# Last value tile in two halves, modulation chunk rows and flips one tile sooner in branch units, modulation straight from the centred tile

## What is computed

```
for l in range(DEPTH):                                    # DEPTH = 2
    sh1, sc1, g1, sh2, sc2, g2 = split(silu(c) @ w_mod[l] + b_mod[l], 6)      # and the same of c_ctx
    a = x * (1 + sc1) + sh1
    f, nq, nk, nv, cq, ckv, kr, g = split(a @ w_in[l])
    ys = [fourier_mix(f), neighbourhood_attention(nq, nk, nv), mla(cq, ckv, kr)]
    m = sum_i(sigmoid(g_i) * (ys_i @ w_branch[l, i])) @ w_out[l]
    x = layer_norm(ALPHA * x + (1 + g1) * m, ln1_g[l], ln1_b[l])
    f = swiglu(x * (1 + sc2) + sh2)
    x = layer_norm(ALPHA * x + (1 + g2) * f, ln2_g[l], ln2_b[l])
```

## Time and profile before

| | |
|---|---|
| median of the 3 runs shown | 2131.55 us (2127.8, 2150.82, 2131.55) |
| profiled execution, its own time | 2127.88 us |
| its span, granted clock (mean) | 2126.1 us, 0.97 |
| PE busy | 1969.0 us (93%), 12468 matmuls |
| PEld (weight loads) | 1626.4 us (76%) |
| VectorE busy | 1281.8 us (60%), 2174 instructions |
| ScalarE busy | 848.6 us (40%), 1366 instructions |
| GpSimd busy | 129.0 us (6%) |
| DMA | 332.07 MB, mean 156 GB/s |

### The profile page before, as it was taken

How to read it: one execution, slowest core, us unless ns; L and a number is a source line. 1 busy time by engine, 2 the same in 40 slices (tenths; PEclk the granted TensorE clock), 3 DMA queues, 4 the chain that set the end, 5 groups by cost and what they waited for, 6 DMA issues and landing times.

```text
span 2126.1 us, 32028 instructions
## 1 busy us (share of the span) xinstructions
PE 1969.0 (93%) x12468; PEld 1626.4 (76%) x12468; DVE 1281.8 (60%) x2174; ACT 848.6 (40%) x1366; POOL 129.0 (6%) x110
## 2 busy tenths in 40 slices
PE   5999989998999999999898988989997899988998
PEld 3776657546768788887687664879997889987998
DVE  6512454564447567677634566666667777666775
ACT  4422353253234122222433445354445754444444
POOL 0000000000030001204000000020111100000000
PEclk9999999999999999999999999999997999998999
DMA  9642513105553556546465140856662446652664
GB/s 328 188 139 82 175 40 94 50 1 181 176 184 123 203 183 200 196 158 218 129 216 167 62 134 2 283 194 196 199 196 90 150 146 193 189 167 81 205 193 137
DMA packets 280758, 332.07 MB, mean 156 GB/s; under 512 B 13190, under 2 KB 229692, under 8 KB 280508
## 3 DMA queue, kind: packets, MB, share of 16 engines
q1 hardware_dynamic: 268608, 323.05, 46.6%
q10 hardware_dynamic: 12028, 7.32, 1.3%
HBM read 329.31 MB, written 1.05 MB: 155 GB/s over the span
## 4 chain that ended last, share of the span: by engine, by line
PE 75%; DVE 8%; issue 6%; DMA 5%; ACT 4%; POOL 1%; SPq 1%; DVEq 0%; ACTq 0%; POOLq 0%
PE ps L550 20%; PE ps L551 19%; PE ps L552 19%; PE ps L1341 3%; DVE SL L509 2%; PE ps L1367 2%; PE ps L368 2%; DMA RAW<-in_w_in 2%; PE ps L1351 2%; ACT SH L503 1%; DMA RAW<-in_w_out 1%; PE ps L947 1%; PE ps L1576 1%; DMA EARLY<-in_w_mod 1%; DMA RAW<-in_w_branch 1%
## 5 line engine op out<-in xcount | busy, mean ns | idle before, releaser
L509 DVE TENSOR_TENSOR SL<-RAW,SH 128x1024 fp32r<-128x1024 f32 (+2 forms) x448 | 524.5, 1174 | 431.1 <-ACT SH L503 426.4
L550 PE MATMUL ps<-AB,SH 128*128 128x256 f32 (+1 forms) x1984 | 644.6, 325 | 40.2 <-DVE AB L1077 22.6
L551 PE MATMUL ps<-AB,SH 128*128 128x256 f32 (+1 forms) x1984 | 637.2, 321 | 0.0
L552 PE MATMUL ps<-AB,SL 128*128 128x256 f32 (+1 forms) x1984 | 636.7, 321 | 0.0
L503 ACT ACTIVATE SH<-RAW 128x1024 fp32r<-128x1024 f32 (+2 forms) x448 | 443.6, 997 | 423.4 <-PE ps L552 269.0
L550 PEld LDWEIGHTS ps<-AB,SH 128*128 128x128 f32 x1984 | 378.2, 191 | 94.4 <-issue 34.5
L552 PEld LDWEIGHTS ps<-AB,SL 128*128 128x128 f32 x1984 | 378.9, 191 | 29.2
L551 PEld LDWEIGHTS ps<-AB,SH 128*128 128x128 f32 x1984 | 378.1, 191 | 27.5
L550 PE MATMUL ps<-HH,SH 128*128 128x256 f32 (+1 forms) x992 | 304.5, 307 | 3.5 <-DVE HL L779 1.6
L551 PE MATMUL ps<-HL,SH 128*128 128x256 f32 (+1 forms) x992 | 302.4, 305 | 0.0
L552 PE MATMUL ps<-HH,SL 128*128 128x256 f32 (+1 forms) x992 | 302.4, 305 | 0.0
(11 more groups left out here) (286 smaller groups left out, 2176.8 us busy)
## 6 DMA issues: line engine op xcount, KB each, us to landing
SIDE<-in_w_mod SPq DMA_DIRECT2D x45, 2048.0 KB, 8.0
RAW<-in_ffn_w SPq DMA_DIRECT2D x64, 1024.0 KB, 5.4
RAW<-in_w_in SPq DMA_DIRECT2D x44, 1024.0 KB, 6.1
RAW<-in_w_ffn_gate SPq DMA_DIRECT2D x22, 1024.0 KB, 9.0
RAW<-in_w_ffn_up SPq DMA_DIRECT2D x22, 1024.0 KB, 5.4
RAW<-in_w_ffn_down SPq DMA_DIRECT2D x16, 1024.0 KB, 5.8
RAW<-in_w_branch SPq DMA_DIRECT2D x24, 512.0 KB, 3.5
RAW<-in_w_out SPq DMA_DIRECT2D x8, 1024.0 KB, 6.7
```

The costliest lines, as they stand in the source:

```text
L509: e.tensor_tensor(SL[:, m, 0:kt, :], RAW[p][:, 0:kt, o:o + P], SH[:, m, 0:kt, :].bitcast(F32), ALU.subtract).then_inc(K.up("weight_low"), 1)
L550: e.matmul(ps, SH[:, m, k, :], xh, start=k == 0, stop=False)
L551: e.matmul(ps, SH[:, m, k, :], xl, start=False, stop=False)
L552: ins = e.matmul(ps, SL[:, m, k, :], xh, start=False, stop=k == self.kt - 1)
```

## The change

Five edits in three groups.

- `Values`: token tile 3 is made in two halves of 256 columns, as tile 0 is. A new semaphore, `values_half`, is signalled after the first half, and ScalarE then splits the next unit's weight tiles 0 and 1 before it copies tile 3 of the values; tiles 2 and 3 follow it.
- Branch units: rows stand before tile 2 (`rows_tile = 2`), and VectorE's flip before it waits for tile 2's products. In the opening, the turn of chunk 2 and the rows of chunk 3 move from before (0, 1) to before (2, 0), and the turn of chunk 3 from before (2, 1) to before (0, 1).
- Norms that write both: A is computed from the centred tile NT, not from X, and ScalarE does so before it writes X. For that the preparation folds gain and bias in: scale = gain x scale', shift = bias x scale' + shift', in DER rows 2, 3 and 8, 9: instead of one VectorE instruction per stream, four. The buffer of NT is still given back after X is written.

```diff
@@ class Unit
+        rows_tile = 3
@@ def pe(self, e, K):
-                if self.side and (m, k) == (3, 0) and not self.by_k:
+                if self.side and (m, k) == (self.rows_tile, 0) and not self.by_k:
                     self.side.pe_rows(e, K, 0)
@@ def dve(self, e, K):
-                if self.side and m == self.side.flip_at and not (self.by_k or self.hold):
+                if self.side and m == (self.rows_tile if self.rows_tile < 3 else self.side.flip_at) and not (self.by_k or self.hold):
                     self.side.flip(e, K, 0)
@@ class Values
-                halves = [(0, 2), (2, 4)] if t == 0 else [(0, 4)]
+                halves = [(0, 2), (2, 4)] if t in (0, 3) else [(0, 4)]
...
+                    if (t, m0) == (3, 0):
+                        ins.then_inc(K.up("values_half"), 1)
                 ins.then_inc(K.up("products"), 1)
...
         def act(self, e, K):
-            for m in range(4):
+            for m in range(3):
                 e.wait_ge(sem["products"], K.at("products", m + 1))
                 self.read_act(e, K, m)
-            for m in range(4):
+            e.wait_ge(sem["values_half"], K.at("values_half", 1))
+            for m in (0, 1):
+                self.nxt.split_act(e, K, m, 2)
+            e.wait_ge(sem["products"], K.at("products", 4))
+            self.read_act(e, K, 3)
+            for m in (2, 3):
                 self.nxt.split_act(e, K, m, 2)
@@ class Branch
+        rows_tile = 2
@@ class Norm, def act
                 t = NT[:, k % 2, c0:c1]
+                if self.to == "a":
+                    if k >= 2:
+                        e.wait_ge(sem["input_low"], K.at("input_low", k - 1))
+                    if self.split and k == 0:
+                        e.wait_ge(sem["dve_done"], K.at("dve_done"))
+                    for s, c in enumerate(range(c0, c1, SEQ)):
+                        last = c + SEQ == c1
+                        at = c - c0
+                        e.activation(A32[:, k % 2, c:c + SEQ], t[:, at:at + SEQ], ACT.Identity,
+                                     bias=self.sh(s, k), scale=self.sc(s, k)) \
+                            .then_inc(K.up("modulated" if last else "act_done"), 1)
                 if self.write_x:
                     e.activation(X[:, k, c0:c1], t, ACT.Identity, bias=self.b(k), scale=self.g(k)) \
                         .then_inc(K.up("x_normed"), 1)
...
-                if self.to == "a":
...
-                    if self.write_x:
-                        e.wait_ge(sem["x_normed"], K.own("x_normed"))
-                        src = X[:, k, c0:c1]
...
+            if self.write_x:
+                e.wait_ge(sem["x_normed"], K.own("x_normed"))
@@ class Opening, def pe_between
-            if (m, k) == (0, 1):
+            if (m, k) == (2, 0):
                 self.turn(e, K, 2)
                 self.rows_of(e, K, 3)
-            if (m, k) == (2, 1):
+            if (m, k) == (0, 1):
                 self.turn(e, K, 3)
@@ 
-    def prep_scales(alpha, mat, chunk_sc, streams):
+    def prep_scales(alpha, mat, chunk, streams, t=slice(0, 8)):
         def f(e, K):
             e.wait_ge(sem["side_added"], K.own("side_added"))
             for s in range(streams):
-                e.tensor_scalar(DER[:, 2 + s, :], mod(mat, chunk_sc, s), 1.0, 1.0 / alpha, ALU.add, ALU.mult) \
+                e.tensor_scalar(DER[:, 2 + s, t], mod(mat, chunk + 1, s)[:, t], 1.0, 1.0 / alpha, ALU.add, ALU.mult) \
                     .then_inc(K.up("dve_done"), 1)
+            e.wait_ge(sem["dve_done"], K.own("dve_done"))
+            for s in range(streams):
+                e.tensor_tensor(DER[:, 8 + s, t], DER[:, 2 + s, t], DER[:, 1, t], ALU.mult).then_inc(K.up("dve_done"), 1)
+            e.wait_ge(sem["dve_done"], K.own("dve_done"))
+            for s in range(streams):
+                e.tensor_tensor(DER[:, 8 + s, t], DER[:, 8 + s, t], mod(mat, chunk, s)[:, t], ALU.add) \
+                    .then_inc(K.up("dve_done"), 1)
+                e.tensor_tensor(DER[:, 2 + s, t], DER[:, 2 + s, t], DER[:, 0, t], ALU.mult).then_inc(K.up("dve_done"), 1)
```

34 lines of the change are left out of this document (9 added, 25 removed).

## The result

The changed kernel takes 2124.69 us in the median of 16 runs (2110.93 to 2134.12). The kernel before, beside it on the same chips, takes 2141.62 us (16 runs, 2127.8 to 2150.95). The ratio is 0.9919, 95% interval 0.9897 to 0.994: 17 us faster. That is 0.8%, less than the 1% from which the prediction would have called it faster. The forecast said 19.1 us, 0.9%. The difference came as forecast, but the time did not: 2124.7 us lies above the range, 2103 to 2120, because the kernel before is slower than the 2128 to 2132 us from which I subtracted.

A forecast was written before the change was run, and what follows sets the result against it. TensorE was taken to bound the kernel (three quarters of the last-ending chain). +0.4 - 2 x 2.5 - 2 x 1.7 - 5.7 - 3.7 - 1.7 = -19.1 us; forecast 2110 (-0.9%), range 2103 to 2120.

The forecast's parts named there:

- Values, -8.4: Tile 3 in halves ends a 2.78 us wait before the gate, costs 0.30; with low clock, 4.2 per layer, 8.4 both.
- echo: Low clock on PE behind a wait, as at 149 to 153 behind Values (0.58), counted at 1.7 us each.
- Branch turns, -5.7: Two branch-unit turns, at 529.38 and 570.46, lose their waits of 2.43 and 3.31 us for the flip: 5.7 us gained.
- Norms, -3.7 and -1.7: A ahead of X gains 0.84, 1.7 and 1.2 us in three norms, together 3.7; clock behind tail waits 1.7 more.
- The half of the echoes that I counted there: Low clock behind two norm-tail waits, 1.7 us each; waits shorten but stay, so 1.7 of 3.4 was counted.
- Opening, +0.4: Six more small VectorE operations make the opening 0.70 us later; one removed wait comes back, leaving a cost of 0.4.
- The 0.27 us that I took back: Opening: one wait of 0.27 us at 52.55 that the earlier turn and rows of chunk 3 would let VectorE remove.
- the NT ring: Rival: norms' centring buffer freed too late, a tile takes 3.3 instead of 2.39 us; +3, 2131; chance 0.04.
- blocked halves: Rival: splits at Values' halves blocked by a bank or RAW, losing 0.6 instead of gaining 8.4; -10, 2118; chance 0.03.
- the second Values' gain given back in layer 1: Rival: layer 1's gate and branch units wait for weights, swallowing 4.2 us; -15, 2114; chance 0.23 with the low-clock rival.
- the low clock moves instead of leaving: Rival: low clock at Values and norm tails only moves, so 3.4 + 1.7 drop out; -14, 2115; 0.23 with the give-back.
- the base: Time the gain was subtracted from: the profiled 2127.88, giving 2108.8; the shown median, 3.7 higher, would give 2112.4.

The follow-up runs named there:

- e5: The kernel before with only the branch units' edit (rows before tile 2, flip before tile 2's products): 2123.11 us, ratio to before 0.9947.
- e6: The changed kernel with the branch units' flip back behind tile 2's products on VectorE, rows still before tile 2: 2119.91 us, ratio to before 0.9915.
- e4: The kernel before with only the norms' part and the opening's moved turns and rows: 2136.06 us, ratio to before 0.9967.
- e8: The changed kernel with the opening's VectorE split of the third weight tile moved behind the first cast: 2120.33 us, ratio to before 0.9916.
- e2: The changed kernel run once more with no edit: 2126.16 us, ratio to before 0.9892.
- e7: The changed kernel with ScalarE writing X ahead of A in each norm tile, A still computed from NT: 2125.04 us, ratio to before 0.9942.
- e3: The kernel before with only Values' token tile 3 in halves and the early splits: 2124.0 us, ratio to before 0.9908.

## Why the prediction was right in the difference and wrong in the time

*Values, -8.4.* Right: 95.8 - 87.4 (8.1 if e5, with its one echo missing, is averaged in). The halves cost 0.31 us in layer 0 and 0.16 in layer 1 (the stretch that ends at the turn went from 24.60 to 24.91 and from 24.60 to 24.76), where I put 0.30 for each. Two waits of 2.78 and two clock echoes are gone.

*Branch turns, -5.7.* Right, 5.9 or 5.3 by the reference, and by the mechanism named (e6). I had too little here: in three of the six profiles that still have these waits, the low clock follows them and costs 1.4 to 4.3 us more ("behind": 50.0, 52.7 and 52.9 in place of 48.6). My remark that these waits have no low stretch behind them was true of one execution. It isn't true of the kernel.

*Norms, -3.7 and -1.7.* Right in the sum: 367.8 to 362.5 is 5.3 us, echoes included, against 5.4. It is spread otherwise than I had it (1.1, 1.6 and 2.5 us in the three), and the tail of layer 0's second norm keeps its echo. In after the clock is low for longer there than the 4 us of the earlier trace rows, and PE still stops for VectorE:

```profile
1030.49 0.38 PE L551 MATMUL ps<-AB,SH 128*128 128x256 f32 x1 [1.76 <-DVE AB L1086]
...
1030.50:1038.00 7.50, 6.99 (x33) 6.67 (x33) 4.19 (x5) 4.69 (x8) 0.00 (x0) 0.54 0.80 167
```

The half of the echoes that I counted there was a guess, and it shows in no row.

*Opening, +0.4.* The chain of small operations was 0.68, forecast 0.70, and it reached PE: from the start of VectorE's reciprocal to PE's first product it is 9.42 us in before (33.19 to 42.61) and 10.09 in after (34.41 to 44.50). The stretches grew by 0.9 on average (71.0 to 71.9, with executions scattered by 1 us). The 0.27 us that I took back were misread: the earlier trace rows has the wait of a weight load. PE's own matmul at 52.55 follows its forerunner by 0.24 us, as its neighbours do, and only its successor comes 0.1 us later than usual. Of the Trainium skill, "VectorE: DVE Perf Modes", section "The DRAIN you can't avoid", I had set aside the rule, measured there on copies, that a semaphore between VectorE operations costs nothing. This trace agrees with setting it aside: six added operations would have taken 0.48 us by it (an estimate, 6 x 0.08) and took 0.68.

*The sum.* By the averages of all profiles: +0.9 - 8.1 - 5.3 - 1.6 (the echoes behind the branch waits) - 5.3 = -19.4 us. Measured as a ratio: -17.3 us, interval -22 to -13. Sum and forecast (-19.1) lie inside. It is partly luck that the terms meet: 1.6 us of echoes that I had put at nothing stand in for what the opening (0.5), the branch turns (0.4) and Values (0.3) fell short. The rivals of the NT ring and of blocked halves are out: no wait for X on VectorE's centring, none at the gate. Nor was the second Values' gain given back in layer 1: the stretch behind is 33.08 us in after, and 33.08 in e4 too, which lacks the edit (32.63 in before and in e8).

*The rival "the low clock moves instead of leaving"* is wrong at the places where I had put it and right in kind elsewhere. The low clock did not move to behind Values. But of the five unfilled profiles with all three parts or nearly so (after, e2, e6, e7, e8) four have a low stretch of 17.1 us at the first attention, and of the other six four have one, of 6.8, 6.8, 13.7 and 17.1 us. One reading of the parts gaining more low clock than the whole is that the whole change meets the long one more often. Five and six profiles are too few to call it shown.

*The step that failed is the base.* "Against the profiled execution's own 2127.88 (span 2126.1 and 1.8 around it) this is 2108.8; the median of the runs shown is 3.7 higher ... I take 2110", and then "a few us for the base being 2127.9 or 2131.6". Three runs were shown, 2127.8, 2131.55 and 2150.82, and I read the first two as the time and the third as an outlier, though it was no less an execution than the others. The median of 112 runs is 2140.4. With it the same sum gives 2121.3, and 2122.5 with the 2141.6 of the runs side by side, 2.2 us from what was measured. The range had to hold the spread of the base, which those three runs showed to be 23 us wide, not "a few us". Beside it, I used the clock of one execution as the clock of the kernel, and did so twice in the sum.

## What to carry to other kernels

Forecast a difference from local rows, and the time from the median of many runs. With three runs that lie 23 us apart, the range has to be as wide as they are, however exact the sum. To judge a change of under 1% in a trace, cut both traces at the same landmarks and compare stretch by stretch: a stretch without low clock repeats to 0.1 us (87.4, 26.8), where whole executions differ by 26 and a stretch with low clock by up to 11. Where many runs list span and granted clock, their product repeats better than the time and shows which part of a difference is the clock. A wait of two or three microseconds on TensorE ahead of dense work was worth more than its length in 7 of 8 cases at Values and 3 of 6 profiles at the branch turns; where it couldn't be removed, a few matmuls into a free bank took away what came behind it.

## What the runs showed of the hardware

- The same program spans 2126.1 and 2151.9 us. PE's loss to the lower clock was 46.0 us in one and 71.7 in the other. Low stretches come up all through the kernel; those followed here, behind stops of 2 to 3 us, are there in some executions and not in others. The Trainium skill, "TensorE: Matmul & The Clock Gate", section "What's actually happening", says that the number of slow matmuls at a kernel's start varies from run to run, with a penalty under 1% of a typical span. That sentence is of the start. The two executions here are 1.2% apart by what happens later, so its figure can't be carried over to the whole kernel.
- Once the lower clock began in the neighbourhood attention, it stayed for 7 to 20 us; in after PE was 98% busy all that time, with score matmuls of 64 rows and transposes (252.5 to 270: 17.23 of 17.50 us, clock 0.51). The 17 us cost the stretch about 4 us (111.0, 110.9 and 111.4 in e8, after and e7, against 107.1 in before and e3), since waits get shorter meanwhile (PE's wait of 0.80 us at 258.99 in before has no counterpart in after). Behind Values it ended after 4 us, under matmuls of 128 rows. What parts the two was not tried.
- At a granted clock of 1.00 TensorE has two paces in long runs of matmuls of 256 columns, 113.3 and 117.8 ns from start to start, each holding for some 160 us. Where it changed, it did so between such runs or near the start of one. PE was busy throughout, a weight load stood beside each matmul, and DMA moved 186 to 194 GB/s at either pace. The cause is open. It is worth 4%, 6 to 7 us each time, and no wait in the profile shows it.
